# Norms summed and inverted with a quarter of the tokens in each quadrant of partitions, and the first attention layer's values weighed earlier

## The chip, the cores and the metric

The kernel runs on one core of a Trainium2 chip. The metric is the device time of one execution in microseconds (us). A core has a matmul engine (TensorE, PE in the profile; its weight loads are listed as PEld), a vector engine (VectorE, DVE), an activation engine (ScalarE, ACT), GpSimd (POOL) and a queue engine (SyncE, SP) that here only starts DMA transfers. The engines run their own instruction streams in order and wait for each other through semaphores. TensorE reads from SBUF, the on-chip memory of 128 partitions, and writes to PSUM, eight banks of 128 partitions x 512 f32 columns.

## The reference

Two blocks over 512 tokens of width 1024, everything in f32. The first block is a mixer (projections, a short convolution, pooling), a feed-forward layer that picks 16 experts per head out of 16384 (PEER), and a gated embedding; the second has two attention layers over the tokens and 256 further context tokens. Each step starts with an RMS norm of its input:

```python
def rms_norm(x, g):
    xf = x.astype(jnp.float32)
    y = xf * lax.rsqrt(jnp.mean(xf * xf, axis=-1, keepdims=True) + EPS)
    return (y * g.astype(jnp.float32)).astype(x.dtype)
```

The names in the kernel are mix, ffn and ple (first block), final (its last norm), a_x and a_ctx (first attention layer, tokens and context), b_x and b_ctx (second attention layer), out (the last one) and three small ones inside the second attention layer.

The first attention layer has 16 heads in 4 key groups. Queries of a block of 128 tokens see the keys of the block before, their own and the next one, and all 256 context keys, with a learned sink in the softmax; context queries see only context keys:

```python
s_loc = jnp.where(m, einsum("bqhgd,bkhd->bhgqk", q, k) * scale, -inf)
s_ctx = einsum("bqhgd,bchd->bhgqc", q, kc) * scale
p = softmax_with_sink(concatenate([s_loc, s_ctx], -1), sink_b)
o = einsum("bhgqk,bkhd->bqhgd", p[..., :384], v) + einsum("bhgqc,bchd->bqhgd", p[..., 384:], vc)
```

## The kernel before

Activations are kept feature-major: a tensor of width 1024 is eight chunks of 128 features (partitions) x 512 tokens (columns). Dense layers are split into units of 128 output features. A unit's weights (512 KB) come by DMA into a ring of four slots; ACT copies them, rounded, into a "high" part (`high_weights`, L942), DVE subtracts to get the "low" part (`low_weights`, L1396), and PE does three passes per chunk (high x high, high x low, low x high; L432 to L434, L410 to L412 when two units are interleaved by `on_x_pair`, L457 to L460 for the context). The normalised input is split the same way: DVE normalises a chunk (`normalise_chunk`, L1406), ACT makes the high part (L965 or L967), DVE the low part (L1415), and PE waits for it chunk by chunk. The order of each engine's stream is written out by hand.

A norm goes like this. ACT squares each chunk (L949) into a ring of three tiles. For mix, ple, a_ctx and the small norms PE multiplies each square by a 128 x 128 matrix of ones and accumulates in one bank (`norm_sums`, L394); that adds over partitions and leaves the sum in all 128 rows. For the norms in `GATHERED` (ffn, a_x, final, b_x, b_ctx, out) POOL adds the squares up first (L1920) and PE does two such matmuls (`gathered_sums`, L400 and L402; for a_x and final together six, L618 to L627). These are plain f32 matmuls. ACT takes the square root of the whole bank (`root`, L957, 128 x 512), DVE the reciprocal (`invert`, L1402, 128 x 512), and then the chunks are normalised with this tile as second operand.

What PE has in its stream behind the sums differs. After mix, ffn and out there is nothing before the normalised chunks. After ple come the embeddings `embed(0..3)` (L590, sixteen f32 passes). After a_x comes `on_context(unit("a_k", 1), 4)`, after b_x `on_context(unit("b_kv", 1), 5)`, and the sums of b_ctx lie in the middle of output unit 6 of the first attention layer, with unit 7 behind it.

The first attention layer works through eight chunks i of two heads each. A chunk has six iterations t: token blocks 0 to 3, then the two context blocks 4 and 5. In an iteration PE issues the scores for the next iteration (`a_scores`, L700, L704, L716), then some pieces of the weighing of values (`a_weigh`), then the transposes of this iteration's probabilities (`a_turn`, L729). The scores wait until ACT has taken the exponentials of the iteration before (L1220, with a read of the row sum behind each). DVE takes the row maxima (L1756), the inverse of the sum (L1761) and scales (L1762); ACT copies the transposed probabilities out of PSUM (L1238 to L1244), and the next transposes wait for that.

A chunk's weighing has eight pieces, all in PSUM bank 6: 0 and 1 (L756, the 256 context keys for all 512 tokens), 2 to 5 (L763, one block of local keys each), then, after DVE has multiplied the result with the gate (`a_gates`, L1777), 6 and 7 (L758, context tokens) and a second gate. Each piece is two matmuls of 64 columns of weights, one for each half of the partitions. `A_PIECES` says which pieces are issued at which t, all of them for the chunk before (i - 1). After the last iteration all eight pieces of chunk 7 follow, and then the output projection.

Of the kernel before, what the change touches and what calls it, by code (L numbers as in the profile page):

```python
# [89 lines left out]

SQUARES = [(name, c) for name in ("mix", "ffn", "ple", "a_ctx") for c in range(KC)]
# [35 lines left out]
def write(nc, d, known):  # L127
# [33 lines left out]
    eps = nc.alloc_sbuf_tensor("eps", [P, 2], F32)  # L161
    ada = nc.alloc_sbuf_tensor("ada", [P, 2, 3, KC, 2], F32)
# [159 lines left out]
    A_PIECES = [(), (0, 1), (2, 3), (4, 5), (), (6, 7)]  # L322
# [64 lines left out]
    def tensor(PE):  # L387
        PE.wait_ge(*at("filled", "eps"))

        def norm_sums(name):  # L390
            chunks, width, b = NORMS[name]
            for c in range(chunks):
                PE.wait_ge(*at("squared", (name, c)))
                PE.matmul(bank[b][:, 0:width], ones[:, :], square(name, c), start=c == 0,  # L394
                          stop=c == chunks - 1).then_inc(*tick("norm_sum", (name, c)))

        def gathered_sums(name):
            chunks, width, b = NORMS[name]
            PE.wait_ge(*at("gathered", (name, chunks - 2)))
            PE.matmul(bank[b][:, 0:width], ones[:, :], sums[name][:, 0:width], start=True, stop=False)  # L400
            PE.wait_ge(*at("squared", (name, chunks - 1)))
            PE.matmul(bank[b][:, 0:width], ones[:, :], square(name, chunks - 1), start=False, stop=True).then_inc(  # L402
                *tick("norm_sum", (name, chunks - 1)))
# [64 lines left out]
        norm_sums("mix")  # L468
        for n in range(16):
# [22 lines left out]
        gathered_sums("ffn")  # L492
        PE.wait_ge(*at("mixed_in", 5))
# [103 lines left out]
        for n in range(4):  # L597
            embed(n)
        on_x_pair(unit("ple"), (0, 1), "ple")
# [10 lines left out]
        def rope(key, dst, b, rows, rot):  # L610
# [5 lines left out]
        (_, _, b), (_, _, bf) = NORMS["a_x"], NORMS["final"]  # L616
        PE.wait_ge(*at("gathered", ("a_x", KC - 2)))
        PE.matmul(bank[b], ones[:, :], sums["a_x"], start=True, stop=False)  # L618
        PE.wait_ge(*at("gathered", ("final", KC - 2)))
        PE.matmul(bank[b], ones[:, :], sums["final"], start=False, stop=False)  # L620
        PE.matmul(bank[bf], ones[:, :], sums["final"], start=True, stop=False)
        PE.wait_ge(*at("squared", ("a_x", KC - 1)))
        PE.matmul(bank[b], ones[:, :], square("a_x", KC - 1), start=False, stop=False)
        PE.wait_ge(*at("squared", ("final", KC - 1)))
        PE.matmul(bank[b], ones[:, :], square("final", KC - 1), start=False, stop=True).then_inc(
            *tick("norm_sum", ("a_x", KC - 1)))
# [1590 lines left out]
```

## Time and profile before

| what | us |
|---|---|
| median of three runs (2501.6 to 2506.83) | 2502.22 |
| the profiled execution | 2506.52 |
| its span, first to last instruction | 2505.1 |
| PE busy in it | 2343.1 |
| DVE busy | 1822.5 |
| ACT busy | 1071.1 |
| POOL busy | 628.6 |

The mean granted TensorE clock of that execution is 0.981 of full speed. The span contains some 33,000 instructions; a timeline row gives its start from the beginning of the span, its length, the engine, the line of the kernel, the operation, the tiles and shapes, and in brackets how long the engine had been idle and which instruction released it. Rows of the same kind that follow each other are merged, with their count (x8). An f32 matmul shows as two rows, one for each pass.

### The profile page before, as it was taken

The numbers are of one execution on the slowest core, as the hardware profiler recorded it, in microseconds if no ns is written. First come the engines' busy times: TensorE is split into PE (matmuls) and PEld (weight loads), VectorE is DVE, ScalarE is ACT, GpSimd is POOL, SyncE is SP. The second block draws the span as 40 slices with busy tenths as digits, with TensorE's granted clock in tenths as the row PEclk, the third lists the DMA queues.
The fourth block names the chain that finished last, engine by engine and source line by source line (L and its number), as shares of the span: only waits on it lengthen the run. The fifth ranks groups of instructions, "written<-read, shape, count | busy, mean of one in ns | idle before, by whom it ended". The sixth has DMA issues, their size and how long they took to land.

```text
span 2505.1 us, 33376 instructions
## 1 busy us (share of the span) xinstructions
PE 2343.1 (94%) x12367; PEld 1982.7 (79%) x12367; DVE 1822.5 (73%) x3390; ACT 1071.1 (43%) x1910; POOL 628.6 (25%) x408
## 2 busy tenths in 40 slices
PE   7989999999999998999999998999788889999997
PEld 5768999999999998999999995688555667555556
DVE  7899898999999977888888876533566555144454
ACT  3332333333388853333333335321466434255552
POOL 4110357787822232333333311100000010000001
PEclk8999999999999999999999999999899999999998
DMA  6537456777889899999999971121000012110001
GB/s 246 193 136 247 165 184 222 250 245 255 263 284 338 311 357 356 366 359 358 371 347 372 341 276 52 51 68 59 18 1 1 26 51 89 63 32 21 12 1 68
DMA packets 162370, 466.72 MB, mean 186 GB/s; under 512 B 15521, under 2 KB 72993, under 8 KB 159777
## 3 DMA queue, kind: packets, MB, share of 16 engines
q1 hardware_dynamic: 100512, 305.19, 34.6%
q0 software_dynamic: 36864, 134.23, 15.1%
q10 hardware_dynamic: 24832, 25.17, 3.1%
q8 instruction: 99, 1.62, 0.3%
q14 instruction: 63, 0.51, 0.1%
HBM read 412.10 MB, written 52.43 MB: 185 GB/s over the span
## 4 chain that ended last, share of the span: by engine, by line
PE 73%; DVE 11%; DMA 5%; ACT 4%; issue 3%; POOL 3%; ACTq 0%; DVEq 0%
PE psum L432 6%; PE psum L576 6%; PE psum L578 6%; PE psum L577 5%; PE psum L433 5%; PE psum L434 5%; PE psum L440 5%; PE psum L442 5%; PE psum L441 5%; DMA arena<-hidden 4%; PE psum L549 3%; POOL weights_low L1960 2%; PE psum L870 2%; PE psum L458 2%; PE psum L885 2%
## 5 line engine op out<-in xcount | busy, mean ns | idle before, releaser
L942 ACT ACTIVATE weights_high<-arena 128x1024 fp32r<-128x1024 f32 x355 | 374.6, 1056 | 426.0 <-PE psum L578 290.4
L1396 DVE TENSOR_TENSOR weights_low<-arena,weights_high 128x1024 fp32r<-128x1024 f32 x266 | 333.9, 1256 | 212.9 <-ACT weights_high L942 211.8
L440 PE MATMUL psum<-x_high,weights_high 128*128 128x384 f32 x1024 | 352.9, 345 | 27.5 <-POOL weights_low L1960 18.1
L576 PE MATMUL psum<-hidden_high,weights_high 128*128 128x384 f32 x1024 | 344.5, 336 | 12.0 <-DVE hidden_low L1658 10.2
L442 PE MATMUL psum<-x_high,weights_low 128*128 128x384 f32 x1024 | 345.1, 337 | 0.0
L441 PE MATMUL psum<-x_low,weights_high 128*128 128x384 f32 x1024 | 344.9, 337 | 0.0
L578 PE MATMUL psum<-hidden_high,weights_low 128*128 128x384 f32 x1024 | 342.9, 335 | 0.0
L577 PE MATMUL psum<-hidden_low,weights_high 128*128 128x384 f32 x1024 | 342.8, 335 | 0.0
L432 PE MATMUL psum<-x_high,weights_high 128*128 128x512 f32 x696 | 278.2, 400 | 23.9 <-DVE weights_low L1396 19.0
L1960 POOL TENSOR_TENSOR weights_low<-arena,weights_high 128x1024 fp32r<-128x1024 f32 x89 | 227.2, 2552 | 204.3 <-ACT weights_high L942 203.8
L434 PE MATMUL psum<-x_high,weights_low 128*128 128x512 f32 x696 | 273.0, 392 | 0.0
L433 PE MATMUL psum<-x_low,weights_high 128*128 128x512 f32 x696 | 273.0, 392 | 0.0
L1954 POOL DMA_INDIRECT arena<-in_v_rows,arena x128 | 153.1, 1196 | 377.6 <-DVE arena L1609 342.2
L440 PEld LDWEIGHTS psum<-x_high,weights_high 128*128 128x128 f32 x1024 | 194.2, 190 | 43.8 <-issue 40.3
L576 PEld LDWEIGHTS psum<-hidden_high,weights_high 128*128 128x128 f32 x1024 | 192.8, 188 | 16.2 <-DVE weights_low L1396 13.4
L1954 POOL DMA_INDIRECT arena<-in_u_rows,arena x128 | 157.9, 1234 | 185.8 <-DVE arena L1593 170.8
L1593 DVE SCALAR_TENSOR_TENSOR arena<-arena 128x1024 f32<-128x1024 f32 x128 | 183.1, 1432 | 17.7 <-DMA arena<-in_u_rows,arena 17.7
L441 PEld LDWEIGHTS psum<-x_low,weights_high 128*128 128x128 f32 x1024 | 194.4, 190 | 0.0
L442 PEld LDWEIGHTS psum<-x_high,weights_low 128*128 128x128 f32 x1024 | 193.9, 189 | 0.0
L577 PEld LDWEIGHTS psum<-hidden_low,weights_high 128*128 128x128 f32 x1024 | 192.8, 188 | 0.0
L578 PEld LDWEIGHTS psum<-hidden_high,weights_low 128*128 128x128 f32 x1024 | 192.7, 188 | 0.0
L1054 ACT ACTIVATE arena<-psum 128x384 f32<-128x384 f32 x128 | 62.7, 490 | 298.5 <-PE psum L442 276.9
(238 smaller groups left out, 4152.6 us busy)
## 6 DMA issues: line engine op xcount, KB each, us to landing
arena<-in_stream SPq DMA_DIRECT2D x227, 512.0 KB, 4.1
arena<-in_v_rows SPq DMA_DIRECT2D x128, 512.0 KB, 7.6
arena<-in_ada_w SPq DMA_DIRECT2D x48, 512.0 KB, 3.4
hidden<-arena SPq DMA_DIRECT2D x128, 192.0 KB, 4.7
router<-arena SPq DMA_DIRECT2D x12, 2048.0 KB, 9.8
arena<-hidden SPq DMA_DIRECT2D x128, 192.0 KB, 8.4
arena<-router ACTq DMA_DIRECT2D x16, 1536.0 KB, 22.1
arena<-in_pair_w SPq DMA_DIRECT2D x8, 640.0 KB, 3.9
```

Of the source, the lines that this page charges most:

```text
L432: PE.matmul(out, wh[w][:, k, 0:m], rh[:, k, 0:n], start=k == order[0], stop=False)
L433: PE.matmul(out, wh[w][:, k, 0:m], rl[:, k, 0:n], start=False, stop=False)
L434: last = PE.matmul(out, wl[w][:, k, 0:m], rh[:, k, 0:n], start=False, stop=k == order[ks - 1])
L440: PE.matmul(bank[b][:, 0:N], wh[u % 2][:, k, :], xh[:, k, PICKED:T], start=k == 0, stop=False)
L441: PE.matmul(bank[b][:, 0:N], wh[u % 2][:, k, :], xl[:, k, PICKED:T], start=False, stop=False)
L442: last = PE.matmul(bank[b][:, 0:N], wl[u % 2][:, k, :], xh[:, k, PICKED:T], start=False, stop=k == KC - 1)
L576: PE.matmul(out, wh[w][:, n, :], hh[:, r, :], start=e == 0, stop=False)
L577: PE.matmul(out, wh[w][:, n, :], hl[:, r, :], start=False, stop=False)
L578: last = PE.matmul(out, wl[w][:, n, :], hh[:, r, :], start=False, stop=e == KEYS - 1)
L942: ACT.activation(wh[u % 2], slots[u % RING], AF.Copy).then_inc(*tick("weights_high", u))
L1396: DVE.tensor_tensor(wl[u % 2], slots[u % RING], wh[u % 2].bitcast(F32), ALU.subtract).then_inc(*tick("weights", u))
L1954: POOL.indirect_dma_start(rows[j % ROW_RING], None, d[f"{table}_rows"], bass.IndirectOffsetOnAxis(ap=chosen[:, entry:entry + 1].bitcast(U3 ...
```

## The change

It does two things.

First, for the seven norms named in the new table `SPREAD` (mix, ffn, ple, a_x, b_x, b_ctx, out) the sum over partitions is made by four matmuls instead of one (`sum_up`): each takes 32 columns of ones and a quarter of the tokens, and writes to one quadrant of 32 partitions. The four quarters of the tokens then lie beside each other in partitions, so root and reciprocal handle a quarter of the columns (128 of 512, 64 of 256 for b_ctx). To get back, `spread` does four matmuls after the reciprocal: the weights are a column of `first_of`, which is 1 in the first row of one quadrant and 0 elsewhere, broadcast to 128 columns; each copies its quadrant's row to all 128 partitions for its quarter of the tokens, into the bank that `SPREAD` names. DVE waits for it and reads the factor from that bank in PSUM instead of from SBUF. The call stands in PE's stream directly behind the sums for mix, ffn and out; behind the four embeddings for ple; behind `on_context(unit("a_k", 1), 4)` for a_x; behind output unit 6 for b_ctx; behind `on_context(unit("b_kv", 1), 5)` for b_x. The norms final, a_ctx and the three small ones keep the old way. The first up unit of the PEER layer waits for the last normalised chunk of ffn instead of its root, because the spread factor is in its bank. POOL fills `first_of` at the start with five small memsets.

Second, in the first attention layer pieces 0 and 1 of a chunk are issued in its own iteration 5 (the sixth block), and the others in iterations 0, 1 and 2 of the next chunk instead of 2, 3 and 5. Piece 0 waits for the probabilities of blocks 0 to 3 only; the wait for blocks 4 and 5 moves to piece 6. The two gates move on DVE to iterations 2 and 3, ahead of the maxima. After the last iteration six pieces are left.

```diff
+SPREAD = {"mix": 4, "ffn": 4, "ple": 2, "a_x": 2, "b_x": 6, "b_ctx": 7, "out": 1}
...
+    first_of = nc.alloc_sbuf_tensor("first_of_quadrant", [P, 4], F32)[:, :]
...
-    A_PIECES = [(), (0, 1), (2, 3), (4, 5), (), (6, 7)]
+    A_PIECES = {5: (0, (0, 1)), 0: (1, (2, 3)), 1: (1, (4, 5)), 2: (1, (6, 7))}
...
+        def sum_up(name, what, start, stop):
+            width, b = NORMS[name][1:]
+            if name not in SPREAD:
+                return PE.matmul(bank[b][:, 0:width], ones[:, :], what, start=start, stop=stop)
+            part = width // 4
+            for g in range(4):
+                last = PE.matmul(bank[b][32 * g:32 * g + 32, 0:part], ones[:, 0:32], what[:, g * part:(g + 1) * part],
+                                 start=start, stop=stop)
+            return last
...
+        def spread(name):
+            part = NORMS[name][1] // 4
+            if name == "mix":
+                PE.wait_ge(*at("filled", "first"))
+            PE.wait_ge(*at("rstd", name))
+            for g in range(4):
+                last = PE.matmul(bank[SPREAD[name]][:, g * part:(g + 1) * part], first_of[:, g:g + 1].to_broadcast([P, P]),
+                                 inverse[name][:, 0:part], start=True, stop=True)
+            last.then_inc(*tick("spread", name))
...
         norm_sums("mix")
+        spread("mix")
...
         gathered_sums("ffn")
+        spread("ffn")
...
-                PE.wait_ge(*at("rooted", "ffn"))
+                PE.wait_ge(*at("normed", ("ffn", KC - 1)))
...
         for n in range(4):
             embed(n)
+        spread("ple")
         on_x_pair(unit("ple"), (0, 1), "ple")
...
         on_context(unit("a_k", 1), 4)
+        spread("a_x")
...
             if piece == 0:
                 for half in range(2):
-                    PE.wait_ge(*at("prob_t", ("a", 12 * i + 10 + half)))
+                    PE.wait_ge(*at("prob_t", ("a", 12 * i + 6 + half)))
...
             elif piece == 6:
+                for half in range(2):
+                    PE.wait_ge(*at("prob_t", ("a", 12 * i + 10 + half)))
                 PE.wait_ge(*at("a_gated", (i, 0)))
...
-            if i:
-                for piece in A_PIECES[t]:
-                    a_weigh(i - 1, piece)
+            back, pieces = A_PIECES.get(t, (0, ()))
+            if i >= back:
+                for piece in pieces:
+                    a_weigh(i - back, piece)
             a_turn(j)
-        for piece in range(8):
+        for piece in range(2, 8):
             a_weigh(7, piece)
...
             chunk(unit("a_out", 6), 0, k, None, k == 0, k == KC - 1)
+        spread("b_ctx")
         for k in range(KC):
             chunk(unit("a_out", 7), 2, k, None, k == 0, k == KC - 1)
...
         on_context(unit("b_kv", 1), 5)
+        spread("b_x")
...
         gathered_sums("out")
+        spread("out")
...
+            if name in SPREAD:
+                width //= 4
             ACT.activation(inverse[name][:, 0:width], bank[b][:, 0:width], AF.Sqrt, bias=bias, scale=scale).then_inc(
...
-            one = inverse[name][:, 0:NORMS[name][1]]
+            width = NORMS[name][1]
+            one = inverse[name][:, 0:width // 4 if name in SPREAD else width]
             DVE.wait_ge(*at("rooted", name))
             DVE.reciprocal(one, one).then_inc(*tick("rstd", name))
-            DVE.wait_ge(*at("rstd", name))
+            if name in SPREAD:
+                DVE.wait_ge(*at("spread", name))
+            else:
+                DVE.wait_ge(*at("rstd", name))
...
+            by = bank[SPREAD[name]] if name in SPREAD else inverse[name]
             DVE.scalar_tensor_tensor(normed_at(name, c), norm_src[name][:, c, :], gain_of(name, c),
-                                     inverse[name][:, 0:NORMS[name][1]], ALU.mult, ALU.mult).then_inc(
+                                     by[:, 0:NORMS[name][1]], ALU.mult, ALU.mult).then_inc(
...
-            if i >= 2 and t == 0:
-                a_gates(i - 2, 1)
+            if i and t in (2, 3):
+                a_gates(i - 1, t - 2)
             if j + 2 < A_JOBS:
                 a_maxima(j + 2)
                 a_maxima(j + 3)
-            if i and t == 4:
-                a_gates(i - 1, 0)
-        a_gates(6, 1)
         a_gates(7, 0)
         a_gates(7, 1)
```

## Rows read from the trace of the kernel before

**Rows 1.** The page, part 4: the chain that ended last, shares by engine.

```profile
PE 73%; DVE 11%; DMA 5%; ACT 4%; issue 3%; POOL 3%; ACTq 0%; DVEq 0%
```

**Rows 2.** One line's instructions, the reciprocal L1402 (ns min/median/max, first and last start).

```profile
L1402 DVE RECIPROCAL rstd<-rstd x8: 3345/3352/3353, 16.8 to 2493.6; 128x512 f32<-128x512 f32 x8
L1402 DVE RECIPROCAL arena<-arena x4: 1745/1753/3343, 1541.2 to 2104.2; 128x256 f32<-128x256 f32 x3, 128x512 f32<-128x512 f32 x1
```

**Rows 3.** The same view of L957, the square root on ACT.

```profile
L957 ACT ACTIVATE rstd<-psum,eps x8: 685/688/690, 15.4 to 2492.8; 128x512 f32<-128x512 f32 x8
L957 ACT ACTIVATE arena<-psum,eps x4: 469/474/688, 1540.5 to 2103.7; 128x256 f32<-128x256 f32 x3, 128x512 f32<-128x512 f32 x1
```

**Rows 4.** The same view of L756, its loads of 64 columns of weights.

```profile
L756 PEld LDWEIGHTS psum<-arena x64: 132/137/231, 1813.8 to 1968.3; 128*64 128x64 f32 x64
```

**Rows 5.** Timeline, norm "mix" (start us, us, engine, line, operation, count, [idle before]).

```profile
5.55 9.74 PE L394 MATMUL psum<-square,ones 128*128 128x512 f32 x16 [5.55 <-ACT square L949]
12.81 0.63 ACT L949 ACTIVATE square<-arena 128x512 f32<-128x512 f32 x1 [0.23 <-PE psum L394]
14.50 2.36 DVE L1396 TENSOR_TENSOR weights_low<-arena,weights_high 128x1024 fp32r<-128x1024 f32 x2 [14.50 <-ACT weights_high L942]
20.16 1.42 DVE L1406 SCALAR_TENSOR_TENSOR arena<-arena,vec,rstd 128x512 f32<-128x512 f32 x2
```

**Rows 6.** Timeline, norm "ffn".

```profile
176.24 1.42 DVE L1406 SCALAR_TENSOR_TENSOR arena<-arena,vec,rstd 128x512 f32<-128x512 f32 x2
```

**Rows 7.** Timeline, norm "ple".

```profile
1509.35 7.03 PE L590 MATMUL psum<-arena 128*128 128x512 f32 x16
1513.66 1.42 DVE L1406 SCALAR_TENSOR_TENSOR arena<-arena,vec,rstd 128x512 f32<-128x512 f32 x2
```

**Rows 8.** Timeline, norm "a_x".

```profile
1597.17 0.39 PE L458 MATMUL psum<-ctx_both,weights_high 128*128 128x512 f32 x1
1598.07 0.75 DVE L1406 SCALAR_TENSOR_TENSOR arena<-arena,fin_gain,rstd 128x512 f32<-128x512 f32 x1
```

**Rows 9.** Timeline, norms "b_ctx" and "b_x".

```profile
2037.65 0.39 PE L412 MATMUL psum<-x_high,weights_low 128*128 128x512 f32 x1
2037.68 0.88 DVE L1406 SCALAR_TENSOR_TENSOR arena<-arena,ada 128x256 f32<-128x256 f32 x2
2057.24 0.40 PE L458 MATMUL psum<-ctx_both,weights_high 128*128 128x512 f32 x1
2059.06 0.75 DVE L1406 SCALAR_TENSOR_TENSOR arena<-arena,ada,rstd 128x512 f32<-128x512 f32 x1
```

**Rows 10.** Timeline, norm "out".

```profile
2497.01 2.08 DVE L1406 SCALAR_TENSOR_TENSOR arena<-arena,vec,rstd 128x512 f32<-128x512 f32 x3
```

**Rows 11.** Timeline, first attention layer, chunk 1, iterations 1 and 0.

```profile
1813.82 1.94 PE L756 MATMUL psum<-arena 128*64 128x512 f32 x8
1815.69 1.31 PE L729 MATMUL psum<-con,arena 128*128 128x128 f32 x10
1816.25 0.20 ACT L1220 ACTIVATION_READ_ACCUMULATOR arena<-psum,small 128x1 f32 x1
1816.93 0.70 PE L700 MATMUL psum<-arena 64*128 64x256 f32 x4
1834.76 0.70 PE L700 MATMUL psum<-arena 64*128 64x256 f32 x4 [1.83 <-ACT arena L1220]
```

**Rows 12.** Timeline, end of the first attention layer.

```profile
1967.38 1.94 PE L756 MATMUL psum<-arena 128*64 128x512 f32 x8 [0.79 <-ACT arena L1241]
```

**Rows 13.** The chain of waits, weighing of three chunks in a row.

```profile
1813.89 1.87 PE psum L756 x8
1836.54 1.87 PE psum L756 x8
1860.62 2.01 PE psum L756 x8
```

**Rows 14.** Busy time in a stretch (us, PE, PEld, DVE, ACT, POOL, clock, DMA).

```profile
1858.00:1860.00 2.00, 2.00 (x9) 0.90 (x6) 0.05 (x1) 0.37 (x2) 0.00 (x0) 0.50 0.00 0
```

More of the change, by code:

```diff
@@ L388, in tensor @@
         PE.wait_ge(*at("filled", "eps"))
+        def sum_up(name, what, start, stop):
[7 more added lines that the diff above has]
+            return last
         def norm_sums(name):
[L391 removed]
+            chunks = NORMS[name][0]
             for c in range(chunks):
                 PE.wait_ge(*at("squared", (name, c)))
[L394 to L395 removed]
+                sum_up(name, square(name, c), c == 0, c == chunks - 1).then_inc(*tick("norm_sum", (name, c)))
         def gathered_sums(name):
[L398 removed]
+            chunks, width, _ = NORMS[name]
             PE.wait_ge(*at("gathered", (name, chunks - 2)))
[L400 removed]
+            sum_up(name, sums[name][:, 0:width], True, False)
             PE.wait_ge(*at("squared", (name, chunks - 1)))
[L402 to L403 removed]
+            sum_up(name, square(name, chunks - 1), False, True).then_inc(*tick("norm_sum", (name, chunks - 1)))
+        def spread(name):
[7 more added lines that the diff above has]
+            last.then_inc(*tick("spread", name))
         def chunk(u, b, k, parts, start, stop):
@@ L614, in tensor @@
         on_context(unit("a_k"), 0, parts="a_ctx")
-        (_, _, b), (_, _, bf) = NORMS["a_x"], NORMS["final"]
         PE.wait_ge(*at("gathered", ("a_x", KC - 2)))
-        PE.matmul(bank[b], ones[:, :], sums["a_x"], start=True, stop=False)
+        sum_up("a_x", sums["a_x"], True, False)
         PE.wait_ge(*at("gathered", ("final", KC - 2)))
-        PE.matmul(bank[b], ones[:, :], sums["final"], start=False, stop=False)
-        PE.matmul(bank[bf], ones[:, :], sums["final"], start=True, stop=False)
+        sum_up("a_x", sums["final"], False, False)
+        sum_up("final", sums["final"], True, False)
         PE.wait_ge(*at("squared", ("a_x", KC - 1)))
-        PE.matmul(bank[b], ones[:, :], square("a_x", KC - 1), start=False, stop=False)
+        sum_up("a_x", square("a_x", KC - 1), False, False)
         PE.wait_ge(*at("squared", ("final", KC - 1)))
-        PE.matmul(bank[b], ones[:, :], square("final", KC - 1), start=False, stop=True).then_inc(
-            *tick("norm_sum", ("a_x", KC - 1)))
-        PE.matmul(bank[bf], ones[:, :], square("final", KC - 1), start=False, stop=True).then_inc(
-            *tick("norm_sum", ("final", KC - 1)))
+        sum_up("a_x", square("final", KC - 1), False, True).then_inc(*tick("norm_sum", ("a_x", KC - 1)))
+        sum_up("final", square("final", KC - 1), False, True).then_inc(*tick("norm_sum", ("final", KC - 1)))
         PE.wait_ge(*at("ple_gated", 4))
         on_context(unit("a_k", 1), 4)
+        spread("a_x")
         PE.wait_ge(*at("sigmoid", 7))
@@ L1908, in gpsimd @@
         POOL.memset(eps[:, 1:2], EPS * EPS)
+        POOL.memset(first_of, 0.0)
         POOL.memset(eps[:, 0:1], EPS).then_inc(*tick("filled", "eps"))
+        POOL.wait_ge(*at("filled", "eps"))
+        for g in range(4):
+            last = POOL.memset(first_of[32 * g:32 * g + 1, g:g + 1], 1.0)
+        last.then_inc(*tick("filled", "first"))
+        POOL.wait_ge(*at("filled", "first"))
         def gather(name, c):
```

## The prediction

> **What bounds the kernel now.** I read first the chain of waits by engine [rows 1]: TensorE (PE) holds 73% of it and VectorE (DVE) 11%. So most microseconds are matmuls that this change doesn't touch, and it can win only where PE stands still on the path: in the seven norms, and in the first attention layer. Then each norm in the timeline [rows 5 to 10], where the reader is to see how long after the last sum the first scalar_tensor_tensor (called the first normalisation below) starts, and what PE does meanwhile. Last the attention layer, at the iterations where PE does not wait [rows 11] and where it does [rows 12 to 14].
>
> **A norm, instruction by instruction.** Reciprocal: 3.35 us for 512 columns and 1.75 for 256 [rows 2], so 6.3 ns a column and 0.95 us for 128: 2.4 us less. Root: 0.69 and 0.47 us [rows 3], so 0.36 for 128 columns: 0.33 less. For b_ctx (256 columns, now 64) the two save 1.2 and 0.16. Added: a semaphore to PE and back, and four f32 matmuls of 128 columns. An f32 matmul is two passes; ten passes of 128 columns take 1.31 us [rows 11], 0.12 each at the full clock, and the last one lasts some 0.27, so eight passes with both signals are 1.15 us; at half the clock (1.2 GHz) about 2. Where PE is idle, the spread norm therefore gains 2.4 + 0.33 - 1.15 = 1.6 us, at the low clock 0.75. Reading the second operand from PSUM I price at nothing: no row shows a difference, and I leave 0.1 us an instruction either way in the range (0.8 us a norm).
>
> The sums. Today a full-width f32 matmul of 512 columns is two passes of 0.43 us (sixteen in 7.03 [rows 7]), 0.86 together. It becomes eight passes of 128 columns on a quarter of the array each. Call its price s. If four quarters run at once and nothing else counts, s = 0.21. If passes are issued one behind the other, s = 8 x 0.12 = 0.95. What speaks for overlap: the two 64-column halves of L756 do eight passes of 512 columns in 1.94 us [rows 11], where one after the other they would need 8 x 0.43 = 3.4. I take s = 0.5, near the middle, since quarters should overlap as halves do, but their passes are so short that issue and weight loads show.
>
> The Trainium skill, "TensorEngine Tiling (Array Packing)", section Key Properties, says that changing the tiling mode drains TensorE. That speaks against the change: each group of sums is now a switch there and back. No row isolates the price. By the rule there are some 14 switches, which at the length of a short pass (0.27 us) would cost up to 3.8 us on the path, where I put nothing beyond s.
>
> **Norm by norm** (gain +, time of the first normalisation before from the rows):
> - mix: +2.0. The sums occupy 5.55 to 15.3, the first ones at half rate [rows 5]. If they keep that length, the reciprocal still starts after DVE's rounding of the weights (14.50 + 2.36 = 16.86), ends at 17.8, and a spread at the low clock gives 19.8 against 20.16: +0.4. If the sums follow the squares (0.63 us each), root and rounding come about 3.5 us earlier: +3.9. I take the middle.
> - ffn: +1.1. PE idle, reciprocal held up to the same moment by DVE's rounding, so only 2.4 - 1.15 = 1.25 counts, with a little for the clock; before: 176.24 [rows 6].
> - ple: a loss, -1.4. Here PE isn't idle: behind the sums it runs the embeddings L590, 7.03 us from 1509.35 [rows 7], while the reciprocal and first halves are prepared, and the first normalisation starts at 1513.66. The spread stands in PE's queue behind those embeddings. Eight sums at s up to 0.63 are paced by the squares and let the embeddings start 2.3 us earlier; they then end at 1513.9, the spread at 1515.05. With s = 0.95 nothing is given back: -4.1.
> - a_x: +0.4. Six sums precede a context projection whose last matmul starts at 1597.17 [rows 8]; four of the six become s. 4 x 0.36 = 1.4 earlier, so it ends at about 1596.1; with the spread's 1.15 that is 1597.3, and I add 0.3 for the two full-width sums of "final" that now stand between narrow ones: 1597.6 against 1598.07. With s = 0.95: -1.2.
> - b_ctx: -0.5. The spread waits until PE has finished output unit 6 (last matmul 2037.65), whereas the first normalisation was at 2037.68 [rows 9]. The sums give back 0.35; four matmuls of 64 columns take 0.8 to 0.9. What follows, x_out(6), the rounding of the b_kv weights and PE's next context projection, all hang on DVE, so it is on the path. The bound is -0.9 without help from the sums.
> - b_x: +1.0. PE ends its context projection at 2057.5 (2057.24 starts the last matmul), 0.7 earlier with s; plus 1.15: 2058.0 against 2059.06 [rows 9]. With s = 0.95: +0.2.
> - out: +1.9. PE idle; 1.6 and 0.3 from shorter sums, before 2497.01 [rows 10]. At the low clock +1.0.
> Sum: 2.0 + 1.1 - 1.4 + 0.4 - 0.5 + 1.0 + 1.9 = **+4.5 us**; with s = 0.95: -2.9 (mix 0.4, ffn 1.0, ple -4.1, a_x -1.2, b_ctx -0.9, b_x 0.2, out 1.7). The memsets at the start lie under the load of x. What follows a norm is a chain of the same engines, so a shift is kept.
>
> **Attention.** Work is only moved. A chunk has six iterations: scores on PE, row maxima on DVE, two exponentials on ACT, the next scores; the weighing pieces lie on PE between scores and transposes. In iteration 1 pieces 0 and 1 (1.94 us) are followed at once by ten transposes (1815.69 + 1.31) and the next scores at 1816.93, while ACT's exponentials were done at 1816.25 + 0.20 = 1816.45 [rows 11]: PE bounds it. With pieces 4 and 5, 0.6 us shorter, it is bound by ACT: gain 0.3. Iteration 2 gets pieces 6 and 7 (256 columns) for 2 and 3 (256 and 384), iteration 3 loses its pieces; in both ACT's exponentials and evictions stand close behind PE, so I give them 0.2 together, an estimate with 0 and 0.8 as ends. Iterations 5 and 0, where pieces 0 to 3 go, are paced by maxima and exponentials, with PE idle before the next scores: 1.83 us in iteration 0 (1834.76 [rows 11]) and a little less in iteration 5. The 1.3 and 0.9 us more that they get fit, just. If they don't, it costs 0.2 a chunk. So 0.5 a chunk, seven chunks: 3.5 (bounds 0 and 6).
> The moved waits: piece 0 now waits for the evictions of iteration 3, piece 6 for 4 and 5 and for DVE's first gate, which DVE can finish only behind two normalisations of the same iteration. Behind piece 6 stand ten transposes and the next scores, for which DVE's maxima wait; that is the tightest spot.
> The tail: after the last iteration pieces 0 and 1 (1.94 us, waiting 0.79 on an eviction [rows 12]) are gone, since 2 to 5 start when they started; less 0.2 because pieces 0 and 1 now stand ahead of the last transposes: +1.75.
> The clock: weighing starts at 1813.89, 1836.54, 1860.62 [rows 13]: 22.65 and 24.08 apart. The longer chunk has the granted clock at 0.50 (1.2 GHz) between 1858 and 1860 [rows 14], right after iterations 5 and 0, where PE had little work; of the six such distances two are long. The change puts 2.2 us of PE work into just that stretch. I take it that both falls go: 2 x 1.4 = +2.8.
> Sum: 3.5 + 1.75 + 2.8 = **+8.1 us**.
>
> **Total** 12.6 us. The profiled execution took 2506.52 us (span 2505.1 and 1.4 around it), so 2493.9 for that one; it was 4.3 above the median of 2502.22, and the parts don't depend on that: 2502.2 - 12.6 = **2489.6 us**.
>
> **Rivals.**
> 1. The short passes are issued one behind the other (s = 0.95), and the clock falls stay. For it: 0.12 us is the pace of 128-column passes in every row here; against: the halves' overlap. Norms -2.9, attention 3.5 + 1.75: 2.4 gained, to 5.2 if the falls go: about 2498. Chance 0.17.
> 2. The attention is only rearranged: maxima and exponentials pace every iteration, gates late in iteration 2 hold piece 6, the clock still falls. Only the tail remains: 4.5 + 1.75 = 6.3: 2495.9. Chance 0.15.
> 3. Slower. The loads of the quarter weights aren't hidden: each pass costs 0.137 (a load of 64 columns [rows 4]) + 0.107 = 0.24, s = 1.95. Place: the sums, mix and ple above all, eight in a row. mix -5, ffn 0, ple -8 x 1.1 - 3.4 = -12, a_x -5.2, b_ctx -2, b_x -1.8, out +0.7: -25; attention +8: 17 slower, 2519. It decides from s about 1.2, where the norms lose 8. Against: in L756 the loads lie under the passes, but its passes are four times as long. Chance 0.08.
> The Trainium skill's same page, Restrictions, lists Fast Weight Load as disabled by column tiling, which would be this rival's cause; here a 64-column load is seen to take 0.137 us, no longer than others.
>
> **How the numbers follow.** Forecast 0.60, with its own range 2485.5 to 2494 (s 0.3 to 0.7, mix 0.4 to 3.9, clock). A measurement tells 0.2%, 5 us, from no change. Faster by more: 0.59 + 0.13 of rival 2 + 0.05 of rival 1 = 0.77; same: 0.15; slower: 0.08. The range 2484.5 to 2500 leaves out rival 3, the ends of the forecast's case and a part of rival 1.
>
> **What would show it.** Root about 0.36 and reciprocal 0.95 us. Eight passes of a quarter sum within 0.5 us, near 0.95 for rival 1, near 2 for rival 3. In ple the spread right behind the last embedding, and PE idle 2 us after it. In b_ctx the spread between output units 6 and 7. Weighing of chunks 22.1 us apart throughout, clock 1.00 in all of them. PE before piece 6 without a wait on DVE. It is wrong if the gap between spread and first normalisation is over 0.2 us, if normalisations take more than 0.75 us each with PSUM as source, or if gains at mix are eaten by the arrival of weights.

## The result, and the profile after

| what | before | after |
|---|---|---|
| median in the same comparison, us | 2501.91 (6 runs) | 2485.64 (6 runs) |
| ratio, 95% interval | | 0.9923 [0.9907, 0.9939] |
| profiled execution / its span | 2506.52 / 2505.1 | 2486.12 / 2484.7 |
| mean granted TensorE clock | 0.981 | 0.988 |

Faster, as forecast, and by more: the ratio is some 19 us, where 12.6 were forecast, and puts the time at about 2483 on the scale of 2502.22, below the end of the range at 2484.5. The interval of that ratio is 15 to 23 us. The changed kernel timed once more gave 0.9933 [0.9918, 0.9948], some 17 us.

How the traces are compared: ACT executes the same 1717 activations in the same order in every kernel here. The start of each in the one trace minus its start in the other says how far ahead the changed kernel is at that point; the difference of two such numbers is what a stage gained.

The norms first, in the timeline after, in the order of [rows 5 to 10] (start us, us, engine, line, operation, count, [idle before]).

```profile
5.56 2.33 PE L401 MATMUL psum<-square,ones 128*32 128x128 f32 x32 [5.56 <-ACT square L979]
8.05 2.46 PE L401 MATMUL psum<-square,ones 128*32 128x128 f32 x32 [0.16 <-ACT square L979]
11.15 2.60 DVE L1428 TENSOR_TENSOR weights_low<-arena,weights_high 128x1024 fp32r<-128x1024 f32 x2 [11.15 <-ACT weights_high L972]
13.66 0.95 DVE L1435 RECIPROCAL rstd<-rstd 128x128 f32<-128x128 f32 x1
14.75 2.05 PE L424 MATMUL psum<-rstd,first_of_quadrant 128*128 128x128 f32 x8 [4.24 <-DVE rstd L1435]
16.84 1.41 DVE L1443 SCALAR_TENSOR_TENSOR arena<-arena,vec,psum 128x512 f32<-128x512 f32 x2 [2.23 <-PE psum L424]
168.11 0.35 ACT L989 ACTIVATE rstd<-psum,eps 128x128 f32<-128x128 f32 x1
170.48 2.08 PE L424 MATMUL psum<-rstd,first_of_quadrant 128*128 128x128 f32 x8 [2.74 <-DVE rstd L1435]
172.59 1.41 DVE L1443 SCALAR_TENSOR_TENSOR arena<-arena,vec,psum 128x512 f32<-128x512 f32 x2 [2.17 <-PE psum L424]
1500.09 7.13 PE L615 MATMUL psum<-arena 128*128 128x512 f32 x16
1501.90 0.94 DVE L1435 RECIPROCAL rstd<-rstd 128x128 f32<-128x128 f32 x1
1507.06 1.05 PE L424 MATMUL psum<-rstd,first_of_quadrant 128*128 128x128 f32 x8
1508.15 1.41 DVE L1443 SCALAR_TENSOR_TENSOR arena<-arena,vec,psum 128x512 f32<-128x512 f32 x2 [5.30 <-PE psum L424]
1510.43 0.47 PE L433 MATMUL psum<-x_high,weights_high 128*128 128x512 f32 x1 [2.32 <-DVE x_low L1452]
1590.51 1.05 PE L424 MATMUL psum<-rstd,first_of_quadrant 128*128 128x128 f32 x8
1591.60 1.40 DVE L1443 SCALAR_TENSOR_TENSOR arena<-arena,fin_gain,psum 128x512 f32<-128x512 f32 x2 [3.34 <-PE psum L424]
1594.03 0.47 PE L433 MATMUL psum<-x_high,weights_high 128*128 128x512 f32 x1 [2.47 <-DVE x_low L1452]
2019.84 1.00 PE L424 MATMUL psum<-arena,first_of_quadrant 128*128 128x64 f32 x8
2020.88 0.87 DVE L1443 SCALAR_TENSOR_TENSOR arena<-arena,ada,psum 128x256 f32<-128x256 f32 x2 [2.82 <-PE psum L424]
2040.56 1.05 PE L424 MATMUL psum<-rstd,first_of_quadrant 128*128 128x128 f32 x8
2041.65 1.41 DVE L1443 SCALAR_TENSOR_TENSOR arena<-arena,ada,psum 128x512 f32<-128x512 f32 x2 [2.41 <-PE psum L424]
2475.47 1.16 PE L424 MATMUL psum<-rstd,first_of_quadrant 128*128 128x128 f32 x8 [1.54 <-DVE rstd L1435]
2476.67 4.04 DVE L1443 SCALAR_TENSOR_TENSOR arena<-arena,vec,psum 128x512 f32<-128x512 f32 x6 [1.25 <-PE psum L424]
```

Every norm has the form that was expected: root 0.35, reciprocal 0.95, the spread, and the first normalisation within 0.05 us of its end. In ple the reciprocal is done at 1502.84, yet the spread stands behind the embeddings until 1507.06; DVE sits idle 5.30 us, and PE then 2.32.

The attention layer: the timeline of one chunk's end, pieces 0 and 1 beside the chunk's own last iteration, and the tail, to be held against [rows 11, 12].

```profile
1817.39 0.70 PE L724 MATMUL psum<-arena 64*128 64x256 f32 x4 [0.33 <-ACT arena L1252]
1818.82 1.94 PE L782 MATMUL psum<-arena 128*64 128x512 f32 x8
1820.69 0.66 PE L753 MATMUL psum<-con,arena 128*128 128x128 f32 x4
1821.57 0.70 PE L724 MATMUL psum<-arena 64*128 64x256 f32 x4 [0.22 <-ACT arena L1252]
1946.84 0.70 PE L724 MATMUL psum<-arena 64*128 64x256 f32 x4
1948.81 1.94 PE L782 MATMUL psum<-arena 128*64 128x512 f32 x8
1951.27 2.37 PE L789 MATMUL psum<-arena 128*64 128x256 f32 x16
1954.53 1.08 PE L784 MATMUL psum<-arena 128*64 128x256 f32 x8 [0.89 <-DVE arena L1814]
1957.20 0.47 PE L481 MATMUL psum<-ctx_both,weights_high 128*128 128x512 f32 x1 [1.59 <-DVE ctx_both L1466]
```

Over the stretch of chunks 1 to 7 the clock never falls, unlike in [rows 14] (columns as there), and in the chain of waits (page, part 4) PE has less and DVE more than in [rows 1]:

```profile
1800.00:1950.00 150.00, 129.93 (x852) 78.66 (x850) 107.28 (x273) 100.65 (x331) 0.00 (x0) 1.00 0.00 1
```

```profile
PE 68%; DVE 15%; DMA 6%; ACT 5%; issue 4%; POOL 2%; SPq 0%; DVEq 0%; ACTq 0%
```

The distances from one iteration's scores (L724) to the next, from all their starts, in us. The third of a chunk holds the pieces of iteration 1.

| chunk | before | after |
|---|---|---|
| 0 | 5.47 5.93 5.93 3.86 2.38 2.38 = 25.95 | 5.47 5.93 4.49 3.86 2.38 2.38 = 24.51 |
| 1, 2, 4 to 6 | 4.18 4.49 4.82 3.90 2.88 2.38 = 22.65 | 4.18 4.49 4.48 3.86 2.58 2.38 = 21.97 |
| 3 (and 7) | 4.18 4.49 **6.39** 3.90 2.88 2.38 = 24.22 | as the others |
| tail, last scores to next projection | 12.18 | 10.36 |

### The profile page after: what moved, and what is told of

Read it like the earlier page. It is cut to its first block, busy times and chain, and to the rows that moved or that the text cites. A ratio compares the mean times of both kernels' runs of the same rounds, so it can differ in the third digit from the quotient of the medians.

```text
span 2484.7 us, 33838 instructions
## 1 busy us (share of the span) xinstructions
PE 2332.8 (94%) x12591; PEld 1979.1 (80%) x12591; DVE 1810.9 (73%) x3390; ACT 1068.2 (43%) x1910; POOL 624.5 (25%) x413
## 4 chain that ended last, share of the span: by engine, by line
PE 68%; DVE 15%; DMA 6%; ACT 5%; issue 4%; POOL 2%; SPq 0%; DVEq 0%; ACTq 0%
PE psum L455 6%; PE psum L457 5%; PE psum L456 5%; PE psum L601 5%; PE psum L603 5%; PE psum L602 5%; DMA arena<-hidden 4%; PE psum L463 4%; PE psum L465 4%; PE psum L464 4%; PE psum L574 3%; PE psum L481 2%; PE psum L899 2%; PE psum L914 2%; PE psum L761 2%
## 5 line engine op out<-in xcount | busy, mean ns | idle before, releaser
L463 PE MATMUL psum<-x_high,weights_high 128*128 128x384 f32 x1024 | 352.1, 344 | 24.8 <-POOL weights_low L2000 18.7
L1994 POOL DMA_INDIRECT arena<-in_u_rows,arena x128 | 152.5, 1191 | 197.6 <-DVE arena L1630 183.2
```

Source lines behind the costliest of these rows:

```text
L463: PE.matmul(bank[b][:, 0:N], wh[u % 2][:, k, :], xh[:, k, PICKED:T], start=k == 0, stop=False)
L1994: POOL.indirect_dma_start(rows[j % ROW_RING], None, d[f"{table}_rows"], bass.IndirectOffsetOnAxis(ap=chosen[:, entry:entry + 1].bitcast(U3 ...
```

## The experiments

What each stage gained against the first profile of before, in us, from the aligned activations. The bounds are points of that profile: up to 189, 1501, 1530, 1599, 1801, 1974, 2098, 2463, end; columns skip 1530 to 1564 and 1599 to 1700, where nothing is over 1.0. Each row is one profile.

| kernel | mix, ffn | PEER | ple | a_x | chunk 0 | attention, rest | b_ctx, b_x | layer b | out | whole span |
|---|---|---|---|---|---|---|---|---|---|---|
| after | 2.8 | 3.3 | -1.0 | 1.5 | 1.4 | 9.7 | -0.2 | 0.6 | 2.2 | 20.4 |
| after, again | 3.2 | -0.3 | -0.6 | 1.5 | 1.4 | 9.8 | 0.0 | 0.6 | 2.2 | 17.8 |
| norms alone | 2.8 | 10.0 | -0.8 | 1.5 | 1.4 | 1.5 | 0.4 | -1.6 | 2.2 | 17.3 |
| moved weighing alone | 0.0 | 6.9 | 0.0 | 0.0 | 0.6 | 9.8 | 0.5 | 0.7 | 0.0 | 19.4 |
| before, again | -0.3 | 4.6 | 0.0 | 0.0 | 0.5 | -0.3 | -1.9 | -0.1 | 0.0 | 3.5 |
| sums twice | 2.0 | -3.6 | -1.4 | 0.6 | 1.4 | 9.6 | -0.7 | -0.2 | 1.9 | 9.0 |
| five norms | 3.1 | 11.4 | -1.3 | 1.5 | 1.3 | 9.5 | 0.4 | 0.6 | 2.2 | 28.5 |
| pieces later | 2.9 | 8.1 | -0.6 | 1.5 | 1.5 | -6.6 | 0.1 | -1.9 | 2.2 | 7.4 |
| pieces later, filled | 2.5 | 6.8 | -1.0 | 1.5 | 1.4 | 1.8 | 0.1 | -1.7 | 2.2 | 13.5 |
| early spreads | 2.8 | 6.1 | 2.8 | 3.5 | 0.0 | 9.8 | 2.7 | 0.6 | 2.2 | 30.7 |
| early, b_ctx full width | 3.7 | -3.8 | 2.8 | 3.5 | 0.0 | 9.6 | 1.6 | -0.2 | 1.3 | 19.1 |

**Norms alone, and moved weighing alone.**

```diff
-    A_PIECES = {5: (0, (0, 1)), 0: (1, (2, 3)), 1: (1, (4, 5)), 2: (1, (6, 7))}
+    A_PIECES = [(), (0, 1), (2, 3), (4, 5), (), (6, 7)]
```

That is norms alone (with the loop, waits and gates of before); the other has the changed attention and no line of the norms' change.

> The seven spread norms alone, the first attention layer as before. Theory 'parts' (each part gives what the aligned traces show at its own place): mix 3.35, ffn 0.35, ple -1.0, a_x 1.5, b_ctx and b_x -0.15, out 2.2, so 6.3 us below before, 2495.7; the PEER stage shows before's length within 0.5 us, since its 2.5 us of gain would then be chance. Rival 'knock-on': an earlier start moves the PEER stage's transfers and half-rate stretches, and the 2.5 us there (and 0.6 near 2440) come again in this kernel: 9.3 us, 2492.7, with the PEER stage 2.5 us shorter than before. My forecast had 4.5 us: 2497.4. Chunk 0 of the attention keeps its 25.95 us if the moved pieces shortened it, and has 24.5 if the earlier start of the stage did.

> The moved weighing and gates alone, all norms as before. Theory 'parts': chunks 21.97 us apart without long ones (7 x 0.68 + 2 x 1.57 = 7.9) and 1.8 in the tail: 9.7 us below before, 2492.2, chunk 0 at 25.95 as before. Rival: the chunk 0 gain of 1.44 belongs to the moved pieces too: 11.1 us, 2490.8. Rival: the two long chunks were in before by chance of the clock and the moved pieces don't remove them: 6.6 us, 2495.3, with one or two iterations of 6.4 us left. The PEER stage must have before's length within 0.5 us if its gain comes from the spread norms; any other length shows how far it wanders by itself, as nothing ahead of it differs from before.

Norms alone: 0.9969 [0.9957, 0.9981], some 8 us. Moved weighing alone: 0.9947 [0.9933, 0.9962], some 13 us, with the 9.7 of "parts" just inside the interval (9.5 to 17). "Parts" holds: each part gives in its own kernel what it gives in the changed one, to some 0.2 us where the clock does not enter, and nothing where it was left out. (On the way to 189 the moved weighing alone was 0.8 us ahead behind mix and lost it again, though nothing ahead of it had changed: so much can be chance there.) "Knock-on" falls: with the weighing alone, whose instructions up to the attention are those of before, the PEER stage came out 6.9 us shorter. Chunk 0's 1.4 us came with the norms; the 1.5 in the rest of their attention is one long chunk instead of two.

**Before again, and after again.** No edit.

> The kernel before once more, with a profile: a shift of nothing against its first profile in mix, ffn, ple, a_x and out (within 0.1), and some us of difference over the PEER stage, if that stage wanders by itself as the run with the moved weighing alone has it (6.9 us there with the same instructions up to that point). In the attention: one or two long chunks again, if the order of before brings the clock's falls; none, if they were chance.

> The changed kernel once more, with a profile. What is the change's own must come again within 0.2 us against the first profile of before: 2.8 at the start of the PEER stage, -1.0 over ple, 1.5 over a_x, 9.7 from chunk 1 of the attention to its end, 2.2 at out, 15.2 in all. What was chance may differ by some us: the PEER stage (2.5 to 3.3 in the first profile), the half-rate stretch in chunk 0 (1.44), the one near 2440 (0.6). If the PEER stage's gain is the change's own, it comes again as 2.5 to 3.3.

The change's own came again (2.8 and 3.2, -1.0 and -0.6, 1.5, 9.7 and 9.8, 2.2), chunk 0's 1.4 too, but the PEER stage's 3.3 did not (-0.3), and before again is 4.6 shorter there. Over the twelve profiles the stage ranges over 15 us. DVE waits there for gathered rows; the view of waits between 190 and 1490 us (total, times, longest), of before, of five norms (11.4 us shorter) and of sums twice (3.6 longer):

```profile
DVE arena L1653 <- DMA arena<-hidden: 37.4, 28, 4.0
```

```profile
DVE arena L1688 <- DMA arena<-hidden: 23.6, 21, 3.1
```

```profile
DVE arena L1691 <- DMA arena<-hidden: 43.9, 22, 5.6
```

The five profiles with at most 30 us of such waits gained 6.8 to 11.4 there, the seven with more 6.1 at most. That goes together and is not a proof, and why the transfers arrive later in one execution than in another was not tested. Before again has two long chunks too (1 and 5). The stage of b_ctx and b_x differs by 1.9 us between the two profiles of before.

**Sums twice**, the price of a quartered sum.

```diff
-            for g in range(4):
-                last = PE.matmul(bank[b][32 * g:32 * g + 32, 0:part], ones[:, 0:32], what[:, g * part:(g + 1) * part],
-                                 start=start, stop=stop)
+            for again in range(2):
+                for g in range(4):
+                    last = PE.matmul(bank[b][32 * g:32 * g + 32, 0:part], ones[:, 0:32], what[:, g * part:(g + 1) * part],
+                                     start=start and not again, stop=stop and again == 1)
```

> The changed kernel with every quartered sum issued twice (the sums come out doubled, so the norms scale otherwise; the work is the same). It prices one quartered sum, s. On the path are the last sum of ple and mix, four of a_x, one or two each of ffn, b_ctx, b_x and out: about 11. Theory 'quarters overlap', s = 0.2: 1 to 2.5 us slower than the changed kernel, two sums of 16 passes take no more than 0.45 us of PE. My forecast's s = 0.5: 5.5 us slower. One behind the other, s = 0.95: over 10 us slower, and the sums of ple no longer keep pace with squares 0.52 us apart.

2492.24 us, 0.994 [0.9922, 0.9958]. The aligned stages give 2.9 for mix, ffn, ple, a_x, b and out together against the first profile of the changed kernel and 3.9 against the second, more than the 1 to 2.5 expected; eleven sums at the price below are 2.8. The timeline at ple prices the sum itself:

```profile
1504.21 4.18 PE L402 MATMUL psum<-square,ones 128*32 128x128 f32 x128
1508.33 7.13 PE L616 MATMUL psum<-arena 128*128 128x512 f32 x16
```

Sixteen sums in 4.12 us, one after the other with no idle: s = 0.257, or 0.032 a pass, at the full clock. "Quarters overlap" holds, though two sums take 0.51 and not 0.45 at most; my 0.5 for one was twice too large and rival 1's 0.95 nearly four times.

**Five norms**: ffn and b_ctx full width again.

```diff
-SPREAD = {"mix": 4, "ffn": 4, "ple": 2, "a_x": 2, "b_x": 6, "b_ctx": 7, "out": 1}
+SPREAD = {"mix": 4, "ple": 2, "a_x": 2, "b_x": 6, "out": 1}
```

> The changed kernel with ffn and b_ctx computed full width again, five norms spread. My forecast: ffn's spread brings 1.1 us, b_ctx's costs 0.5, so the aligned trace is 1.1 us later at the start of the PEER stage (a shift of 1.7 in place of 2.8 against before) and 0.5 earlier by the end of b_x. What the trace of the changed kernel suggests: ffn's spread brings nothing, since the rounding of weights ahead of the reciprocal sets its time (shift 2.8 kept within 0.3), and b_ctx costs 0.9 at its first normalisation, all or part of which is given back by b_x's wait.

2478.0 us, one execution. The shift at the start of the PEER stage is 3.1, against 2.8 and 3.2 with ffn's spread: what it brings does not show there, where 1.1 was forecast. At the first normalisation of ffn the spread does bring 0.3: every kernel that has it steps ahead by 0.3 to 0.5 there, this one does not. In the stage of b_ctx and b_x it is 0.4 against -0.2 and 0.0, but norms alone, which has b_ctx's spread, is at 0.4 too; so the stage does not show the forecast 0.5. What shows is that at its first normalisation b_ctx loses 0.95 with its spread and nothing here.

**Early spreads.**

```diff
         for n in range(4):
+            if n == 2:
+                spread("ple")
             embed(n)
-        spread("ple")
...
+        spread("a_x")
         on_context(unit("a_k", 1), 4)
-        spread("a_x")
```

The same for b_x, and b_ctx's spread ahead of the last part of output unit 6.

> The changed kernel with four spreads put earlier in PE's queue: ple between the second and third embedding, a_x and b_x ahead of the context projection, b_ctx ahead of the last part of output unit 6. Theory 'the spread's place in the queue is the loss': ple +2.1 (embeddings run while DVE normalises; PE's 2.3 us idle ahead of the projection goes), a_x +1.6 and b_x +1.6 (2.47 idle after the spread against 1.3 idle ahead of it), b_ctx +0.6: 5.9 us below the changed kernel, 2479.7. Rival: DVE's rounding of weights ahead of the norms holds them, and nothing but ple's 1 to 2 us comes: 2484.

2475.92 us, 0.9888 [0.9873, 0.9904]: faster than both kernels, the intervals don't touch. ple turns from -1.0 to +2.8, a_x from 1.5 to 3.5, b from -0.2 to 2.7: 8.7 us more, where 5.9 were expected; chunk 0 gives its 1.4 back. Part of what b gains is the clock: over the 30 us behind b_ctx's norm the granted clock is 0.83 after (2030 to 2060) and 0.94 here (2023 to 2053). By the ratios this kernel is 9 to 11 us faster than the changed one. The timeline at ple shows how:

```profile
1497.30 3.70 PE L615 MATMUL psum<-arena 128*128 128x512 f32 x8
1500.83 1.05 PE L424 MATMUL psum<-rstd,first_of_quadrant 128*128 128x128 f32 x8
1501.72 3.60 PE L615 MATMUL psum<-arena 128*128 128x512 f32 x8
1501.93 1.41 DVE L1445 SCALAR_TENSOR_TENSOR arena<-arena,vec,psum 128x512 f32<-128x512 f32 x2 [1.87 <-PE psum L424]
1504.76 0.79 PE L433 MATMUL psum<-x_high,weights_high 128*128 128x512 f32 x1
```

DVE normalises under the second half of the embeddings, and the projection follows them without idle.

**Pieces later, then filled.** All pieces one iteration later, the gates too; then the same with work that nobody reads in the empty iteration (the lines from `if t == 5`).

```diff
-    A_PIECES = {5: (0, (0, 1)), 0: (1, (2, 3)), 1: (1, (4, 5)), 2: (1, (6, 7))}
+    A_PIECES = {0: (1, (0, 1)), 1: (1, (2, 3)), 2: (1, (4, 5)), 3: (1, (6, 7))}
...
+            if t == 5:
+                for n in range(8):
+                    rows = slice(64 * (n % 2), 64 * (n % 2) + 64)
+                    PE.matmul(bank[7][rows, 256:512], vt[:, 4, 0:64], vt[:, 0, 0:256], start=True, stop=True)
```

> The changed kernel with all eight weighing pieces one iteration later than it has them: none beside the chunk's own last iteration, 0 and 1 in the next chunk's iteration 0, 2 and 3 in 1, 4 and 5 in 2, 6 and 7 in 3, each gate one iteration later, and all eight behind the last chunk. Theory 'PE no longer bounds an iteration': iteration 1 keeps 4.48 us (its 640 columns are as many), iterations 2 and 3 stay within 0.2, chunks stay 22.0 to 22.4 us apart, and only the tail's 1.85 us is lost: 2 to 4 us slower than the changed kernel. Theory 'two iterations with little PE work let the clock fall': the last iteration is empty again, but iterations 2 to 4, once empty in part, are filled; a half-rate stretch (an iteration of 6.0 us or more in place of 4.5) comes in one or more chunks, 1.6 us each. Rival: no falls, as they hang on how the stage lies in time and not on the pieces.

> The kernel with all pieces one iteration later, and in its empty last iteration of each chunk eight f32 matmuls of 256 columns that nobody reads, at the place where the changed kernel has pieces 0 and 1 and of the same length (1.94 us). It adds work and moves none. Theory 'PE work there holds the clock': the half-rate stretches, five in seven chunks without it, go or fall to one, 1.6 us each, and the work itself lies in PE's idle time: 6 to 8 us faster than without it, about 2492.5. Rival 'what matters is which piece stands where': the long iterations of 6.1 us stay, time 2499.6 or some us more.

Later: 2499.63 us, 0.9994 [0.9979, 1.0008], so the attention is 6.6 us slower than before instead of 9.7 faster, where a loss of 2 to 4 us was expected. Five of seven chunks have an iteration of 6.1 to 6.2 us; without it a chunk takes 22.88 (0.73 of the 0.91 more come from pieces 6 and 7 in iteration 3). Filled: 2492.25 us, 0.9961 [0.9946, 0.9977]: more work, and about 8 us faster. No chunk has a long iteration any more, each takes 22.86. Busy time by stretch of iterations 4, 5 and 0 (us, PE, PEld, DVE, ACT, POOL, clock, DMA), later first:

```profile
1787.50:1789.90 2.40, 1.38 (x10) 0.73 (x9) 1.71 (x8) 2.25 (x9) 0.00 (x0) 1.00 0.00 0
1789.90:1794.10 4.20, 1.97 (x14) 1.44 (x15) 2.80 (x10) 2.12 (x7) 0.00 (x0) 1.00 0.00 0
1794.10:1797.00 2.90, 2.89 (x12) 1.58 (x14) 0.55 (x2) 0.41 (x2) 0.00 (x0) 0.57 0.01 3
```

Of the same kernel, iteration 5 and the start of iteration 0 in one of the two chunks without a long iteration:

```profile
1838.70:1842.90 4.20, 1.97 (x15) 1.44 (x15) 2.80 (x9) 2.12 (x7) 0.00 (x0) 1.00 0.00 0
1842.90:1845.80 2.90, 2.90 (x16) 1.51 (x18) 1.62 (x4) 0.62 (x3) 0.00 (x0) 1.00 0.00 0
```

Filled:

```profile
1789.90:1792.30 2.40, 1.35 (x10) 0.76 (x9) 1.71 (x7) 2.27 (x9) 0.00 (x0) 1.00 0.00 0
1792.30:1796.50 4.20, 3.99 (x32) 2.56 (x32) 2.80 (x9) 2.13 (x7) 0.00 (x0) 1.00 0.00 0
1796.50:1801.10 4.60, 4.60 (x28) 2.37 (x28) 3.01 (x8) 2.12 (x6) 0.00 (x0) 1.00 0.01 4
```

Behind 1.97 us of PE work in 4.20 the clock is at its lower level (1.2 GHz) for most of the next 2.9 us; behind 3.99 it stays at 1.00. The iteration itself is no longer for the work. So the idle time of PE just before is what lets the clock fall, not which piece stands where: matmuls that nobody reads hold it. But the same 1.97 in 4.20 is followed by 1.00 in two chunks of seven, and before, PE is busy for 2.66 us of these 4.20 both where the clock then falls and where it does not. What decides between such chunks was not tested.

**Early spreads, b_ctx at full width, piece 0 of the last chunk earlier.**

```diff
+            if j == A_JOBS - 4:
+                pieces = (0,)
+            elif j == A_JOBS - 2:
+                pieces = (1,)
```

> The kernel with the spreads put early, with b_ctx computed full width again, and in the last chunk alone piece 0 one iteration earlier, so that 1.94 us less stands just ahead of the last transposes. Theory: b_ctx without a spread is 0.2 to 0.5 us faster by the end of b_x, the tail 0.3 to 0.9 us shorter; the rest as with the early spreads: 2475 against its 2475.9, which the times alone will not tell apart, the aligned traces will. Rival: piece 0 doesn't fit beside iteration 4 (0.71 us idle for 0.97) and delays the last scores by what the tail gains: no change in the attention.

2476.32 us, 0.9883 [0.986, 0.9905]: no better than early spreads. The attention is at 9.6 against 9.8, so the rival holds for the tail. The stage of b_ctx and b_x gained 1.6 against 2.7, where 0.2 to 0.5 more had been expected. That is a miss, but no price of b_ctx's spread: the granted clock over the 30 us behind that norm is 0.89 here and 0.94 with early spreads. At b_ctx's own first normalisation the early spread costs 0.2.

## Why the prediction fell short

| step | forecast | measured |
|---|---|---|
| mix and ffn | 2.0 + 1.1 | 3.2 - 0.2 |
| ple | -1.4 | -0.8 |
| a_x | +0.4 | +1.5 |
| b_ctx and b_x | -0.5 + 1.0 | -0.1 |
| out | +1.9 | +2.2 |
| iterations of chunks 1 to 7 | 3.5 | 4.8 |
| two falls of the clock | 2.8 | 3.1 |
| tail | 1.75 | 1.8 |
| chunk 0 | nothing | 1.4 |
| sum | 12.6 | 16.9 |

Measured is the mean of the two profiles of the changed kernel against before's; the two ratios give 17 to 19 us. The sum leaves out the PEER stage (3.3 and -0.3), which differs as much between profiles of one kernel, and layer b (0.6), where a half-rate stretch of before near 2445 is missing. Where the time gained beyond 16.9 us belongs is not shown. The span shows 20.4 because the first profile of before was long in its PEER stage, where before again was 4.6 us shorter.

The sum was 4.3 us too small, by several terms. Chunk 0 was put at nothing and gave 1.4; the iterations were 1.3 short; a_x was 1.1 short and ple 0.6, for the most part through the price s of a quartered sum; mix was 1.2 short, because I took the middle of two bounds. Against that ffn and b_ctx with b_x were 1.3 and 0.6 too high. The parts of the change work as described, the falls of the clock and the tail to 0.3 us; the level of the clock at ffn was wrong.

**The price s of a quartered sum** is the mis-sized term of the norms: 0.257, not 0.5. The lower bound of 0.21, "four quarters at once and nothing else counts", was close, and I took the middle. At a_x PE is 1.9 us sooner through the sums (rows further down) and not 1.4, and the 0.3 added for the sums of final was not needed: 0.8 of the error of 1.1. At ple the embeddings start 3.1 us earlier (1509.35 [rows 7] to 1500.09, with 6.1 ahead at that point) and not 2.3. At mix the sums keep pace with the squares and end at about 10.5 rather than 15.3 [rows 5]; the rounding of the weights starts at 11.15 rather than 14.50, and all behind it follows: the first normalisation from 20.16 to 16.84, 3.3. The middle of 0.4 and 3.9 was wrong there, the end at which the sums follow the squares nearly right.

**ffn** was priced with a warm spread of 1.15. It took 2.08, since the clock stood at its lower level there, so its first normalisation gained 0.3 (176.24 [rows 6] to 172.59, 3.65, of which mix has 3.3 to 3.4). In the first profile it is lost again by 189, with 0.5 more: the clock stays low until 180.2 there, 183.9 on the scale of before, where before it rises at 181.5. In the second profile 0.2 of it are left. The price at the lower clock was in the text. The trace before would not have said surely which one applied:

```profile
174.00:176.00 2.00, 0.00 (x0) 0.00 (x0) 2.00 (x1) 0.00 (x0) 0.00 (x0) 0.68 0.00 0
```

Up to 174 its clock is 1.00, and a short reciprocal would have ended at about 173.9.

**b_ctx** starts its normalisation 1.0 later (2037.68 [rows 9] to 2020.88, with 17.8 ahead at that point), near the bound of -0.9 that I had given for no help from the sums. The sums did help, by 0.3. But the spread takes 1.04 until the normalisation starts, and not 0.8 to 0.9, and it waits for the end of a matmul that started at 2037.65, 0.2 behind the old start. **b_x** made up 0.6 of it, and not 1.0; the clock over the 30 us there was granted at 0.83, against 0.89 before.

**The iterations.** Their bound was read rightly (iteration 1: 4.82 to 4.48, 0.34 against 0.3), but iteration 3, where pieces 4 and 5 delayed the transposes, gave 0.30 alone and not "0.2 together" with iteration 2, which gave 0.04. So 0.68 a chunk instead of 0.5. PE is not what bounds the last iterations of a chunk now: ahead of the scores it waits for ACT's exponentials (0.33 and 0.22 in the rows above).

**Chunk 0.** At the start of the stage the clock is at its lower level in all kernels (0.50 from 1777 to 1792 before, and until 1781 after, where the stage starts at 1770.9), and the long distances end with the second or with the third: 24.5 to 24.8 us in the seven profiles of kernels whose a_x norm stands where the change puts it, 25.4 to 25.95 in the three with before's norms and the two with early spreads. So it goes with the norms ahead of the stage, not with the pieces that were moved into it. What exactly decides it, such as how the stage's start lies in time, was not tested.

**The rule on draining.** The Trainium skill, "TensorEngine Tiling (Array Packing)", Key Properties, says that a change of tiling mode drains TensorE; by it I gave up to 3.8 us. The rows put two sums between passes of full width:

```profile
2037.10 0.42 PE L401 MATMUL psum<-gathered,ones 128*32 128x128 f32 x8
2037.34 0.40 PE L401 MATMUL psum<-square,ones 128*32 128x128 f32 x8
2037.68 0.50 PE L481 MATMUL psum<-ctx_both,weights_high 128*128 128x512 f32 x1
```

From 2037.10 to 2037.68 are 0.58 us, of which 2 x 0.257 are the sums: 0.07 remain for the way back to full width. The way in costs as well. At a_x two groups of narrow sums stand among full-width passes; the last context pass ahead of all six sums and the first behind them, after and then before:

```profile
1584.24 0.40 PE L481 MATMUL psum<-ctx_both,weights_high 128*128 128x512 f32 x1
1587.33 0.79 PE L481 MATMUL psum<-ctx_both,weights_high 128*128 128x512 f32 x1
```

```profile
1589.24 0.39 PE L458 MATMUL psum<-ctx_both,weights_high 128*128 128x512 f32 x1
1594.21 0.79 PE L458 MATMUL psum<-ctx_both,weights_high 128*128 128x512 f32 x1
```

That is 3.09 us for 4.97, 1.88 less, where four sums at 0.257 in place of 0.86 would make 2.41. So a group costs about a quarter of a microsecond beyond its sums, with both its switches. The kernel has ten such groups, about half of them at places where PE waits for its input anyway; my estimate from these rows is 1 to 2.5 us in the kernel. The trace agrees that a switch costs something; I had put nothing in the sum. Fast Weight Load being disabled (same page, Restrictions) costs nothing that shows: eight loads and passes in 0.257 us rule out rival 3 (s above 1.2). No run shows whether these f32 weights had it at full width.

**Rivals.** 1 fell with s. 2 fell in the attention: 9.7 us, not 1.75. 3 fell with the loads. The normalisation from PSUM takes 0.74 us, as from SBUF [rows 8: 0.75].

## What to carry to other kernels

A wait moved into another engine's queue costs what stands ahead of it there: put the small instruction that releases DVE ahead of independent PE work, even at the price of a short idle of PE, and DVE works under that work (some 9 us here for a few moved lines). When an iteration leaves PE half idle, count the clock as well as the wait: work moved into the hole takes no time of its own and can save a fall of the clock, 1.6 us each here. Where a bound from full overlap and one from none lie far apart, a doubled copy of the instructions, timed in one trace, settles it.

## What the runs showed of the hardware

- Eight f32 passes of 128 columns on a quarter of the array each, with their weight loads, take 0.257 us; one quarter sum alone has 0.42 from start to end.
- Matmuls that nobody reads, put into the iteration in which PE was busy 1.97 of 4.20 us, took all five falls of the clock away and made the kernel about 8 us faster (0.9994 to 0.9961). With the same 1.97 us the clock did not fall in the other two chunks. The Trainium skill, "TensorE: Matmul & The Clock Gate", Part 1, says that the gate follows how busy TensorE has been; these runs agree.
- A stage of 1300 us with the same instructions differs by up to 7 us between profiles of kernels that are alike up to it, so one pair of profiles can't place a gain of that size there.
